# Where projection 0 of a step stands: in pieces inside the inverse of the step before, or as one run of eight matmuls in its own step

## The reference

```python
p = h @ w_in                                    # 5 plain + 3 shifted blocks of 1024 columns, and 256 rank columns
plain, rw = p[..., :N_PLAIN], p[..., N_PLAIN:]
rw = rw + (token_shift(rw) - rw) * token_mu
cb, cc, ch, ga, gb = jnp.split(plain, ...)      # gated short convolution, two gates
r, k, v, wd, ad, gd = jnp.split(rw, ...)        # RWKV-7 branch
...
def step(state, inp):                           # per head, over the tokens
    r_t, w_t, k_t, v_t, kk_t, a_t = inp
    sa = jnp.einsum('bhvk,bhk->bhv', state, kk_t)
    state = (state * w_t[:, :, None, :]
             - sa[..., None] * (kk_t * a_t)[:, :, None, :]
             + v_t[..., None] * k_t[:, :, None, :])
    y = jnp.einsum('bhvk,bhk->bhv', state, r_t)
    return state, y
...
merged = jax.nn.sigmoid(ga) * y_conv + jax.nn.sigmoid(gb) * y_rwkv
return merged @ w_out
```

## Time and profile before

| | |
|---|---|
| time, median of 3 runs | 5508.87 us (5507.02 to 5515.28) |
| the profiled execution | 5513.11 us, of which its span 5511.2 us |
| TensorE matmul busy | 5093.8 us, 92% |
| weight loads (beside matmuls) | 2682.3 us, 49% |
| VectorE busy | 1764.7 us, 32% |
| ScalarE busy | 1415.1 us, 26% |
| L784, the mixer's projections | 2018.8 us busy in 4096 records |
| L872, small batches of the inverse, `Qm,Zm` / `Tm,LTb` | 179.4 / 183.6 us busy in 5120 records each |
| mean granted clock of TensorE | 0.957 |

### The profile page before, as it was taken

One profiled execution on the slowest core, in us unless ns is written; L12 is line 12 of the kernel. 1 busy time (PEld: TensorE's weight loads), 2 busy tenths in 40 slices (PEclk: granted clock), 3 DMA queues, 4 the chain that ended last, 5 costly groups with the idle time before them and its releaser, 6 DMA issues.

```text
span 5511.2 us, 97586 instructions
## 1 busy us (share of the span) xinstructions
PE 5093.8 (92%) x38809; PEld 2682.3 (49%) x38809; DVE 1764.7 (32%) x3775; ACT 1415.1 (26%) x3000; POOL 151.8 (3%) x274
## 2 busy tenths in 40 slices
PE   6699999999999999999999999799599999999970
PEld 1345555555555555555555555445344444444430
DVE  1233434434334334334344343322411111111124
ACT  1613223232232232232232322223111111111115
POOL 0000000000000000000000000000000000000013
PEclk8699999999999999999999999799699999999985
DMA  5110100100100100100100100033488888888865
GB/s 200 65 45 11 41 7 11 41 7 11 41 7 11 41 9 9 41 11 12 37 11 14 34 11 7 35 120 118 155 338 339 329 336 338 338 327 339 337 235 197
DMA packets 252238, 635.90 MB, mean 115 GB/s; under 512 B 10825, under 2 KB 95995, under 8 KB 251902
## 3 DMA queue, kind: packets, MB, share of 16 engines
q1 hardware_dynamic: 238224, 580.70, 29.0%
q0 software_dynamic: 13680, 49.81, 2.6%
HBM read 561.77 MB, written 68.71 MB: 114 GB/s over the span
## 4 chain that ended last, share of the span: by engine, by line
PE 91%; DMA 3%; DVE 3%; ACT 2%; issue 2%; SPq 0%; ACTq 0%; DVEq 0%; POOL 0%; POOLq 0%
PE bank L784 35%; PE bank L1043 16%; PE bank L872 8%; PE bank L1063 8%; PE bank L969 4%; PE bank L865 2%; PE bank L868 2%; PE bank L809 1%; PE bank L818 1%; PE bank L828 1%; PE bank L695 1%; PE bank L1032 1%; PE bank L665 1%; DMA x<-x_s 1%; DMA adaw<-in_w_ada_dram 1%
## 5 line engine op out<-in xcount | busy, mean ns | idle before, releaser
L784 PE MATMUL bank<-hT,w 128*128 (+1 forms) x4096 | 2018.8, 615 | 13.6 <-DMA w<-in_w_in_dram 13.6
L784 PEld LDWEIGHTS bank<-hT,w 128*128 128x128 f32 x4096 | 704.9, 189 | 648.2 <-issue 593.9
L1043 PE MATMUL bank<-WI,xT 128*128 128x512 f32 x2016 | 877.6, 593 | 2.4 <-DVE xT L1830 2.4
L1043 PEld LDWEIGHTS bank<-WI,xT 128*128 128x128 f32 x2016 | 378.8, 190 | 456.1 <-issue 456.1
L1063 PE MATMUL bank<-WO,aT 128*128 128x512 f32 x1008 | 443.1, 592 | 0.7 <-ACT aT L1090 0.7
L1479 DVE SCALAR_TENSOR_TENSOR St<-St,pcs,bank 64x64 f32<-64x64 f32 x512 | 143.3, 280 | 909.5 <-PE bank L830 905.8
L1090 ACT ACT_TABLE_LOAD x291 | 373.4, 1283 | 11.3 <-DVE ub L1587 5.3
L1836 DVE TENSOR_TENSOR gsig<-bank,gsig 128x512 f32<-128x512 f32 x63 | 43.6, 691 | 883.8 <-ACT gsig L1090 883.8
L1063 PEld LDWEIGHTS bank<-WO,aT 128*128 128x128 f32 x1008 | 186.7, 190 | 212.4 <-issue 211.4
L1090 ACT ACTIVATE gsig<-bank 128x512 f32<-128x512 f32 x63 | 37.6, 597 | 821.9 <-PE bank L1043 821.9
L1090 ACT ACTIVATE tok<-bank 128x256 f32<-128x256 f32 x192 | 63.2, 381 | 714.2 <-PE bank L868 714.2
(11 more groups left out here) (308 smaller groups left out, 5023.3 us busy)
## 6 DMA issues: line engine op xcount, KB each, us to landing
WI<-in_w_expert_in_dram SPq DMA_DIRECT2D x63, 4096.0 KB, 17.1
WO<-in_w_expert_out_dram SPq DMA_DIRECT2D x63, 2048.0 KB, 7.9
w<-in_w_in_dram SPq DMA_DIRECT2D x64, 512.0 KB, 4.0
y_s<-ysb SPq DMA_DIRECT2D x63, 512.0 KB, 17.7
adaw<-in_w_ada_dram SPq DMA_DIRECT2D x12, 2048.0 KB, 7.6
xt<-in_x_dram SPq DMA_DIRECT2D x16, 512.0 KB, 3.2
WAc<-rank_s SPq DMA_DIRECT2D x32, 256.0 KB, 3.2
GDc<-rank_s SPq DMA_DIRECT2D x32, 256.0 KB, 3.2
```

The source lines that it names most:

```text
L784: ins = mm(PJ[j % 2][:, :], w[:, j, k, :], hT[:, k, ds(group(i) * G, G)], start=k == 0, stop=k == KT - 1)
L1043: ins = mm(GU[j][:, :], xT[:, s, k, :], WI[:, s, k, j * DE:j * DE + DE], start=k == 0, stop=k == KT - 1)
```

## The change

The table `fill_at` and the pieces in `grams` go, and with them the argument `more`. `head` runs all eight matmuls of projection 0 in one run, behind zaaa and ahead of projection 1, also in the first step. The other engines' programs are the same.

```diff
-            fill_at = {("LT", 0): [0, 1, 2], ("TR", 0): [3], ("TR", 1): [4], ("TR", 2): [5], ("Z", 5): [6, 7]}
-
-            def grams(i, more):
+            def grams(i):
...
                         by_head(i, u, (bank((kind, lv, 0, 0)), bank(u)))
-                        if more and (kind, lv) in fill_at:
-                            proj_part(i + 1, 0, fill_at[kind, lv])
...
                 zaaa(i)
+                proj(i, 0)
                 proj(i, 1, q)
...
-                grams(i, more)
+                grams(i)
...
-            proj(0, 0)
             head(0, None)
```

More of the change, by code:

```diff
@@ L916, in head, with tail @@
                 proj(i, 4)
-            def tail(i, q, more=True):
+            def tail(i, q):
                 if q is not None:
@@ L938, in _ @@
                 head(i + 1, i)
-            tail(STEPS - 1, STEPS - 2, more=False)
+            tail(STEPS - 1, STEPS - 2)
             for c in range(NC):
```

## The result

| | before | changed |
|---|---|---|
| median | 5507.94 us (4 runs, 5506.94 to 5515.28) | 5640.05 us (4 runs, 5637.82 to 5642.07) |
| profiled execution | 5513.11 us, span 5511.2 | 5638.32 us, span 5636.3 |
| mean granted clock | 0.957 | 0.952 |
| ratio to before | | 1.0237, 95% interval 1.0219 to 1.0255 |

The changed kernel is 2.4% slower, 132 us; 5640 had been forecast, 131 us over before.

A forecast was written before the change was run, and what follows sets the result against it. TensorE's order of work and waits were taken to bound the mixer. Per step 6.86 - 0.20 - 3.59 + 1.2 = +4.27 us, times 31, minus 1.1 at the start, gave +131: 5640 us, range 5600 to 5658.

The forecast's parts named there:

- What bounds the kernel: In the mixer, time is TensorE's given work plus its waits; TensorE busy 3069.62 of 3090 us.
- The run of eight: Between zaaa and projection 1, eight matmuls add 6.86 us a step; covering VectorE's state restart saves 0.20.
- The pieces: Removing projection matmuls from each inverse shortens it by 3.59 us at full clock, to 25.98.
- The clock: The 2.4 us wait before the first Zm batch lowers TensorE's clock in most inverses, adding 1.2 us a step.
- The start: Before step 0, zdec and zaaa run inside projection 0's wait for weights: minus about 1 us, once.
- The sum: Whole kernel: +4.27 us a step over 31 steps, minus 1.1 at the start, +131 us: 5640 us.
- B: Clock rarely falls in the loop: 5603 us, or 5594 if loop waits are shorter than the last inverse's; 13%.
- C: VectorE answers in time in the loop, leaving the inverse at TensorE's own work: faster, 5471 us; 2%.
- D: Wait before the inverse's last batch also lowers the clock, slowing part of the eight projections: 5690 us; 5%.

The follow-up runs named there:

- first-piece kernel: Changed kernel with matmuls 0 to 2 of projection 0 back after the LT batch, 3 to 7 run in their own step; 5525.2 us, ratio 1.0027.

## Why the prediction was right

- **What bounds the kernel:** right. TensorE's order and its waits account for all of it.
- **The run of eight, +6.86 a step, less 0.20 at chunk 0:** right. Outside the inverses a step grew by 6.68 us, and the nine projections ahead of chunk 0 read 7.92. The expected gain of the one matmul put there alone (0.20 a step) came as well.
- **The pieces, -3.59:** right to 0.1. It came from one inverse, the last, with the fall taken out of it by hand: 25.98 us. The seven inverses without a fall average 25.91 and those with idle matmuls 25.75. Of the two reasons given for it, the first stands by experiment: the wait for LTb fills 2.4 us in each, and idle matmuls fit into it without moving the Zm batch. The second, that the updates wait for VectorE's masks, is shown at level 2, where moving VectorE's products shortens the distance without pieces and does nothing with them. At level 3 it is not shown; part of the distance there is pauses of TensorE.
- **The clock, +1.2, chosen between 0 and 1.61:** it was 1.30, as 24 falls in 31 at 1.68. The share had been reasoned from two waits of the trace. It could have come out otherwise: the last inverse of the first-piece kernel shows the same wait with no fall, and the other kernels' profiles have 20 to 29 falls. That 1.2 came so near is luck in part. The price of one fall was a little over the bound of 1.61, since the fallen inverses also have more of the pauses named below: Zm to the update of level 1 costs 1.58 us more in them, level 3 another 0.13.
- **The start, -1.1:** right in its direction; its size stays open. zdec and zaaa do run inside the wait for the weights: in the changed kernel they start at 280.52 us, and projection 0 follows at 282.53 with no wait. The prediction counted these two matmuls and nothing else. On average the profiles with the new first step are 2.8 us shorter there than the two with the old one, single ones of each kind differ by some 2 us, and the time of the kernel with that edit alone can't tell -1 from -4 or from nothing.
- **The sum:** a step +4.27 forecast, +4.30 measured. The three terms of a step each came within 0.1 us, so this is not a wrong term made good by another; only the clock's share could not be known.
- **The rivals:** B (no falls) is excluded by the clock rows and by the idle matmuls; had it held, the time would be that of the kernel with them, 5598, near the 5603 given. C (faster) is excluded by the waits. D (a second fall in a step) did not occur: after the wait of 0.94 us at level 5 the run of projections goes on at 0.43 us a record. The rule cited from the Trainium skill, page "TensorE: Matmul & The Clock Gate", section "Why this matters for your kernels", which names idle gaps of about 3 us, does not hold here: 2.4 us, which is less than that, lowered the clock in 24 of 31 inverses, 1.3 us and 0.5 us in none.

## What to carry to other kernels

Price a piece of filling work by the wait it covers where it stands, not by its own length: three matmuls of the projection were worth 115 us behind LT and next to nothing behind the transposes. Look for a place in the kernel that already runs without the thing you would remove (the last turn of a loop, a first one); its rows gave both the new length and the clock's fall. And when TensorE waits some 2 us in each turn of a loop, count the low clock behind the wait too: here it was 40 of the 132 us, and one useless matmul in the wait took it away.

## What the runs showed of the hardware

- The clock falls after some waits and not after others of the same length: in the profiles, after 24 of 31 waits of 2.40 us in the changed kernel, 29 in the kernel with pieces behind the transposes only, 25 in the one with VectorE's products moved, 20 in the one with a pair behind the last Zm.
- Where the clock fell, it did so at another place each time. In three steps in a row of the changed kernel the low clock begins 6.3, 6.0 and 5.2 us behind L (1721.8, 1827.6 and 1933.4), and in the next step there is none. In the kernel with pieces behind the transposes, whose steps are more alike, 20 steps in a row fell, each 4.9 to 5.1 us behind L. So when a wait comes seems to count beside its length; no run changed that alone.
- In most profiles TensorE has a wait in the conditioning stage that ends between 62.3 and 64.3 us, and its length differs from run to run. A low clock followed it within 1 us in all seven profiles where it took 2.03 to 2.29 us, but not in one where it took 2.37, nor in those where it took 1.92 us or less. The prediction had one of the seven.
- Long rows of small matmuls (the changed kernel's inverse has 20 batches without a 128x512 matmul between) show pauses that wait for nothing in the profile, up to 1.0 us, in the lists of waits all of them among the transposes (L868). Zm to update at level 3 reads 2.20 in some inverses and 2.69 in others. In the kernels with a piece at each of these places it reads 3.07 nearly always. So a piece there may also hide some of that. What the pauses are stays open.
